# Norm, gating and transposes of each mixer's result inside its out-projection

## The reference

```python
x = x + gate * rms_norm(sublayer(rms_norm(x, g_pre) * (1 + scale) + shift), g_post)
```

```python
# even mixer: two results, one out-projection over both
y_ssd  = rms_norm((ssd(...) + xh * D) * silu(z), norm_w)              # norm over all 1024
y_diff = rms_norm(diff_attention(...), subln_w) * (1 - lam_init)      # norm over each head of 128
out    = concatenate([y_ssd, y_diff]) @ w_out
# odd mixer: retention, then sliding-window attention
y_ret  = rms_norm(retention(...)) * silu(rg)                          # norm over each head of 256
out    = concatenate([y_ret, y_swa]) @ w_out
```

## Time and profile before

| | us |
|---|---|
| median of 3 runs (3827.09 to 3835.24) | 3834.69 |
| the profiled execution, by its own clock outside | 3826.52 |
| its span in the trace | 3824.7 |
| PE busy in it | 3221.2 (84%) |
| DVE busy in it | 2412.0 (63%) |
| ACT busy in it | 1276.7 (33%) |
| POOL busy in it | 575.5 (15%) |

### The profile page before, as it was taken

How to read it: one execution, slowest core, us unless ns; L and a number is a source line. 1 busy time by engine, 2 the same in 40 slices (tenths; PEclk the granted TensorE clock), 3 DMA queues, 4 the chain that set the end, 5 groups by cost and what they waited for, 6 DMA issues and landing times. The chain is left out here.

```text
span 3824.7 us, 41388 instructions
## 1 busy us (share of the span) xinstructions
PE 3221.2 (84%) x14800; PEld 2569.7 (67%) x14800; DVE 2412.0 (63%) x3816; ACT 1276.7 (33%) x2025; POOL 575.5 (15%) x148
## 2 busy tenths in 40 slices
PE   4999967884799895888379789668999898899999
PEld 4766856663676684766367478546887687667887
DVE  6756576897567667689544736466775564465445
ACT  2223224774323323577222514222111322232111
POOL 0000002432000000343100000102444100003443
PEclk9999988997899997899689799888999999769999
DMA  7653526996644452899552033022443251202232
GB/s 247 215 163 127 176 94 228 338 338 222 211 158 143 169 168 91 288 336 338 195 169 73 17 107 127 5 72 78 154 143 110 99 183 63 94 23 80 96 99 77
DMA packets 289773, 584.47 MB, mean 153 GB/s; under 512 B 26034, under 2 KB 134003, under 8 KB 282414
## 3 DMA queue, kind: packets, MB, share of 16 engines
q1 hardware_dynamic: 277610, 537.42, 42.0%
q10 hardware_dynamic: 7364, 27.81, 1.8%
q0 software_dynamic: 4608, 16.78, 1.2%
HBM read 528.93 MB, written 79.76 MB: 159 GB/s over the span
## 5 line engine op out<-in xcount | busy, mean ns | idle before, releaser
L131 ACT CAST w_hi<-ring 128x2048 fp32r<-128x2048 f32 (+2 forms) x172 | 319.3, 1861 | 1276.8 <-PE ps L280 1100.4
L280 PE MATMUL ps<-hT_hi,w_hi 128*128 128x512 f32 (+1 forms) x1256 | 500.4, 398 | 22.8 <-DVEq L898 10.3
L280 PE MATMUL ps<-hT_lo,w_hi 128*128 128x512 f32 (+1 forms) x1256 | 498.4, 397 | 0.0
L138 POOL TENSOR_TENSOR w_lo<-ring,w_hi 128x2048 fp32r<-128x2048 f32 x64 | 307.1, 4799 | 963.3 <-ACTq L2584 466.8
L143 DVE TENSOR_TENSOR w_lo<-ring,w_hi 128x2048 fp32r<-128x2048 f32 (+3 forms) x112 | 245.2, 2195 | 293.3 <-ACT w_hi L131 293.2
L280 PE MATMUL ps<-hT_hi,w_lo 128*128 128x512 f32 (+1 forms) x1256 | 306.9, 396 | 9.4 <-DVE w_lo L143 9.4
L280 PEld LDWEIGHTS ps<-hT_hi,w_hi 128*128 128x128 f32 (+1 forms) x1256 | 238.5, 190 | 82.3 <-DVEq L898 12.0
L280 PEld LDWEIGHTS ps<-hT_hi,w_lo 128*128 128x128 f32 (+1 forms) x1256 | 237.0, 189 | 66.7 <-DVE w_lo L143 10.9
L837 DVE SCALAR_TENSOR_TENSOR piece_sums<-pieces,cond,piece_sums 128x512 f32<-128x512 f32 x294 | 220.8, 751 | 88.9 <-DMA pieces<-in_w_ada_dram 56.1
L280 PEld LDWEIGHTS ps<-hT_lo,w_hi 128*128 128x128 f32 (+1 forms) x1256 | 238.3, 190 | 55.6
L280 PE MATMUL ps<-w_hi,hT_hi 128*128 128x512 f32 (+1 forms) x672 | 259.9, 389 | 1.0 <-ACT w_hi L131 1.0
(11 more groups left out here) (596 smaller groups left out, 6721.6 us busy)
## 6 DMA issues: line engine op xcount, KB each, us to landing
ring<-in_mlp_w_dram SPq DMA_DIRECT2D x64, 1024.0 KB, 5.2
pieces<-in_w_ada_dram SPq DMA_DIRECT2D x96, 512.0 KB, 5.9
ring<-in_w_in_dram SPq DMA_DIRECT2D x36, 1024.0 KB, 7.3
pieces<-in_mod_w_dram SPq DMA_DIRECT2D x72, 512.0 KB, 5.0
raw_sep<-in_w_exp_gate_dram SPq DMA_DIRECT2D x50, 512.0 KB
raw_sep<-in_w_exp_up_dram SPq DMA_DIRECT2D x50, 512.0 KB
raw_sep<-in_w_exp_down_dram SPq DMA_DIRECT2D x24, 1024.0 KB
ring<-in_e_w_in_dram SPq DMA_DIRECT2D x24, 1024.0 KB, 5.5
```

What stands on the lines that cost most here:

```text
L131: self.k.nc.scalar.copy(self.k.parts[0][:, i, 0:words], self.k.ring[:, i, 0:words]).then_inc(self.high, 1)
L138: self.k.nc.gpsimd.tensor_tensor(self.k.parts[1][:, i, 0:words], self.k.ring[:, i, 0:words], self.k.parts[0][:, i, 0:words].bitcast(F32), ...
L280: mm = pe.matmul(out, a if weight_left else b, b if weight_left else a, start=first and part == 0 and q == ks[0] and o == 0, stop=last and ...
```

## The change

`out_projection`, `last_projection`, `gate_rows`, `column_of` and `head_norm_T` are gone. `norm_projection` is one stage that takes the raw result, norms it row tile by row tile (class `Heads`), and multiplies a tile as soon as it is turned.

- The first two weight halves are loaded at the start of the stage before (`load_ahead` in `diff_attention`, `ssd` and `retention`), and ACT casts both to high there (`round_ahead`): in the middle of the 32 units of the attention and of the 16 of the SSD, and at once in the retention. The scratch of the first two moved out of `ring` into its own space.
- In the new stage DVE makes the low parts of the weights and does, per tile: sum of squares per head (places A and B), reciprocal, scale (and gate), and the low part of the turned tile. ACT squares, takes the root and casts high. PE turns a tile in 8 transposes between the two halves of the tile before.
- No warm-up matmuls are left in these three projections.
- In place C the norm's weights come as a row of 1024 for all partitions, and are applied in the scaling; in A they come as a column of 128 by a DMA inside the projection before (`loads`), and are scaled on DVE at the start of the attention.
- In place C the scale and shift rows are loaded after the last tile is turned, and `hand.rows` moves from between the halves of unit 0 to `by_tile`, after tiles 0 and 1 of unit 1 (`late_rows=0`, banks 0 to 3).

```diff
@@ by_tile
     part(1, 1).then_inc(hand.tile_done, 1)
+    if hand.late_rows is not None:
+        pe.wait_ge(hand.row_landed, 64)
+        pe.wait_ge(hand.step, hand.started)
+        pe.wait_ge(hand.y_out, NT)
+        hand.rows(pe, hand.late_rows)
     part(2, 0)
@@ hand_over_on_scalar
     hand.root_y(act, 1)
+    if hand.late_rows is not None:
+        hand.shift_out(act, hand.late_rows)
     hand.square_x(act, 1)
@@ hand_over_on_vector
     sum_of(1)
+    if hand.late_rows is not None:
+        hand.scale_out(dve, hand.late_rows)
     hand.modulate(dve, 0, link)
...
+def round_ahead(k, act, ahead):
+    for i in range(2):
+        act.wait_ge(k.ahead[i], ahead)
+        k.nc.scalar.copy(k.parts[0][:, i, :], k.ring[:, i, :])
...
+    def scaled(self, dve, t):
+        V, y, m = self.k.nc.vector, self.src[:, t, :], self.ms[:, t, :]
+        dve.wait_ge(self.rooted, t + 1)
+        self.link(V.reciprocal(m, m))
+        if self.row is not None:
+            V.scalar_tensor_tensor(y, y, m, self.row, ALU.mult, ALU.mult).then_inc(self.y_made, 1)
+            return
+        ins = V.tensor_tensor(self.per_head(y), self.per_head(y), bcast(m, 2, D // self.nh), ALU.mult)
+        if self.after is not None:
+            self.link(ins)
+            ins = V.tensor_tensor(y, y, self.after[:, t, :], ALU.mult)
+        ins.then_inc(self.y_made, 1)
...
+def norm_projection(k, w, y, first, heads, ahead, next_ahead, hand_of=None):
...
+        def _(act):
+            act.nop().then_inc(W.high, 2)
+            H.square(act, 0)
+            H.root(act, 0)
+            H.square(act, 1)
+            H.high(act, 0)
+            for t in (1, 2):
+                H.root(act, t)
+                H.square(act, t + 1)
+                H.high(act, t)
+            H.root(act, 3)
+            H.high(act, 3)
+            W.split_high(act, 1, 0, 32)
+            W.split_high(act, 1, 1, 32)
...
+            def part(t, i):
+                pe.wait_ge(H.high_out, t + 1)
+                W.high_ready(pe, 0, i)
+                for a, o in ((0, 0), (0, 1), (1, 0)):
+                    if o:
+                        pe.wait_ge(H.low_out, t + 1)
+                    if a:
+                        W.low_ready(pe, 0, i)
+                    for q in range(half):
+                        mm = pe.matmul(k.ps[:, t, :], out[o][:, half * i + q, t * P:(t + 1) * P], wv[i][a][:, q, :], ...
+            H.turn(pe, 0)
+            for t in range(NT):
+                mm = part(t, 0)
+                if t == NT - 1:
+                    mm.then_inc(W.read, 1)
+                else:
+                    H.turn(pe, t + 1)
+                mm = part(t, 1)
+            mm.then_inc(W.read, 1)
...
+        def _(dve):
+            if hand is not None:
+                hand.start(dve)
+                H.gate_in(dve, 0)
+            W.split_low_on_vector(dve, 0, 0)
+            H.total(dve, 0)
+            if hand is not None:
+                H.gate_in(dve, 1)
+                dve.wait_ge(row_in, 16)
+            H.scaled(dve, 0)
+            W.split_low_on_vector(dve, 0, 1)
+            H.low(dve, 0)
+            for t in range(1, NT):
+                H.total(dve, t)
+                if hand is not None and t + 1 < NT:
+                    H.gate_in(dve, t + 1)
+                H.scaled(dve, t)
+                H.low(dve, t)
...
@@ ssd and diff_attention, ACT, in the loop over the units
+                if i == N // 2:
+                    round_ahead(k, act, ahead)
```

More of the change, by code:

```diff
@@ L670, in last_projection @@
-        hand = Handover(k, c, sems[5:], y, out, xh[:, 0:2 * D].rearrange("p (a d) -> p a d", a=2), zz[:, 3 * D:4 * D].rearrange("p (a n) -> p a n", a=2),
-                        zz[:, 0:3 * D], xh[:, 2 * D:4 * D].rearrange("p (a d) -> p a d", a=2))
-        half = KD // 2
+        out = pair_of(nc, c, "normedT", [P, KD, S])
+        H = Heads(k, c, sems[5:15], out=out, **heads)
+        y_done, row_in = sems[15:17]
+        hand, mod = hand_of(c, sems[17:]) if hand_of is not None else (None, None)
@@ L674, in _ @@
+        row = None
+        if hand is not None:
+            y_done = hand.y_out
+            row = c.enter_context(nc.sbuf_tensor(fresh("norm_row"), [P, D], F32))
+            H.row = row[:]
         @block.sync
@@ L676, in _ @@
             W.came_ahead(sp, ahead)
-            hand.load(sp, *mod)
+            if hand is not None:
+                sp.dma_start(row[:], bcast(heads["row"], 0, P)).then_inc(row_in, 16)
             for i in range(2):
                 W.load(sp, 1, i, [(W.raw(i, half, 512), w[:, half * i:half * (i + 1), 512:1024])])
+            if hand is not None:
+                sp.wait_ge(row_in, 16)
+                sp.wait_ge(H.turned, NT)
+                hand.load(sp, *mod)
             sp.wait_ge(W.low, 6)
@@ L689, in _ @@
             W.split_high(act, 1, 1, 32)
-            hand_over_on_scalar(k, act, hand, ahead + 16)
+            if hand is not None:
+                hand_over_on_scalar(k, act, hand, ahead + 16)
+            else:
+                act.wait_ge(W.high, 4)
         @block.tensor
         def _(pe):
[L694 to L700, removed]
@@ L701, in _ @@
-            token_unit(k, pe, W, src, 0, 0, 512, before=rows)
-            pe.wait_ge(hand.row_out, 2)
-            by_tile(k, pe, W, 1, hand, src, KD)
+            pe.nop().then_inc(W.read, 2)
+            wv = [[W.part(a, i, half, 512) for a in range(2)] for i in range(2)]
+            def part(t, i):
[7 more added lines that the diff above has]
+                    for q in range(half):
+                        mm = pe.matmul(k.ps[:, t, :], out[o][:, half * i + q, t * P:(t + 1) * P], wv[i][a][:, q, :],
+                                       start=i == 0 and a == 0 and o == 0 and q == 0, stop=i == 1 and a == 1 and q == half - 1)
+                return mm
@@ L2483, in _ @@
                     V.tensor_copy(taps[:], k.ps[:, 2, 0:80]).then_inc(taps_out, 1)
[L2486 to L2532, removed]
 def mlp(k, w1, w2, hT, y, ahead, side_of=None, mod=None, next_ahead=None, store=None):
@@ L2783, in _ @@
             sp.wait_ge(in_landed, 64)
+            k.load_ahead(sp, next_ahead)
         @block.gpsimd
```

238 lines of the change are left out of this document (113 added, 125 removed).

## The result

The changed kernel takes 3799.57 us (median of 4 runs, 3789.91 to 3805.18) where the kernel before takes 3834.97 (4 runs, 3827.09 to 3840.24). The ratio is 0.9905, with an interval of 0.9890 to 0.9919: 35.4 us less, where 48.4 were forecast. The profiled execution took 3795.96 us, with a span of 3794.2.

A forecast was written before the change was run, and what follows sets the result against it. PE is saturated behind chains of work before three projections, so shortening these shortens the kernel one for one. 14.7 - 2.7 + 12.3 + 29.9 - 5.8 = 48.4 us less, median 3785, range 3768 to 3806.

The forecast's parts named there:

- A: Norm and out-projection after the attention: first unit ends 38.4 us after the stage can start, instead of 53.1; 14.7 less.
- B: Norm and projection after the retention: first unit ends 41.9 us after the stage can start, instead of 54.2; 12.3 less.
- C: Gating, norm and projection after the SSD: first unit ends at 37.8 us instead of 67.7; 29.9 less, 24.1 net.
- rivals 1 and 4: Rival 1, and a fourth: the SSD's hand-over gives back more, all 3.7 lost in the attention, 3792 us; chance 0.08.
- First units: First 96 products of the projections after attention, retention and SSD: end 14.7, 12.3 and 29.9 us sooner.
- C's sum: First unit after the SSD: 16 us, plus 21.8 for the remaining half tiles and two turns, 37.8 in all.
- C's hand-over: Scale and shift rows behind unit 1's first two tiles: VectorE's work 5.3 us later, slower PE 0.5, 5.8 back.
- The upper bound, 10: Most that the hand-over after the SSD could give back: 8.4 + 1.6 us, all that PE loses.
- Attention: Weight casts on ACT delay the next unit's exponentials by 2.5 us, scaling the norm's column adds 0.2: 2.7 back.
- The casts in the SSD and retention loops: Two casts of 1.86 us on ACT: nothing in the retention, 0 in the SSD, at most 0.5 of 3.7.
- Rival 1: The clock falls in the pauses of A and B for two tiles each: 14 us more, 3799; chance 0.15.

The follow-up runs named there:

- the first trace: The profiled execution of the changed kernel's first four runs: it took 3795.96 us, where the median is 3799.57 us.
- the second: The changed kernel run again without any edit, for a second trace: median 3794.0 us.
- the warm start: Changed kernel plus 12 identity products on TensorE ahead of the first turn in each of the three projections: 3785.9 us, ratio 0.9869.
- the tiles ahead: Changed kernel with VectorE summing, scaling and gating tile t+1 before tile t's low part, ScalarE's square and root equally ahead: 3787.8 us.
- A undone: Changed kernel with the stages for the attention's result back to the old way, casts out of the attention: 3808.0 us, ratio 0.9937.
- B undone: Changed kernel with the stages for the retention's result back to the old way: 3796.4 us, ratio 0.9911.
- C undone: Changed kernel with gating, norm, last projection and modulation rows after the SSD back to the old way, no SSD casts: 3800.9 us, ratio 0.9923.

## Why the prediction was right, and where it was not

- **The number.** 3799.6, 3794.0 and 3795.7 us lie inside the stated range (3768 to 3806) and 9 to 15 above the median of 3785. The places themselves gave what was forecast, in part by errors that cancel. The range, made wide for other reasons (rivals 1 and 4), also held a loss that the prediction had not thought of; that is luck.
- **First units.** A 2.6, B 2.1, C 2.2 us shorter than forecast. In A the chain was sized at 7.4 per tile and PE's work at 6.7; they are below 6.58 and 6.44 (24 x 0.233 + 0.85, since the next products start 0.85 behind a turn's start). The single low part of 1024 elements takes 1.28, where I had two of 512 at 1.55; sum and product take 1.21 and 1.23 instead of 1.25 and 1.35. In C's sum the text says six half tiles and adds seven (7 x 2.8 + 2.2 = 21.8); seven is right.
- **C's hand-over.** Forecast 5.8 back; 5.3 with the clock at 2.4 GHz, 11.5 with it falling in the row matmuls, which two of three traces show. The order on VectorE, the wait (3.95 or 7.60 against "5") and the start of `modulate(0)` (12.3 against 12.4) are as argued. The upper bound, 10, was too low: it let PE run slow only behind the rows, and they cost 3.6 more themselves (12.0 for 8.4); the rest of the difference between 5.3 and 11.5 comes behind them.
- **Attention.** Forecast 2.7 back, measured 3.2 to 3.6. The block of 3.70 us stands on ScalarE at 2138.95, and VectorE waits 2.05 behind it, as the prediction said to look for. The casts in the SSD and retention loops are free, as forecast.
- **The step that failed is one that the prediction took for granted:** that the stages behind a place keep their time. They gave back 18.2 us in the first trace and 13.4 in the second. That they did so at a lower granted clock is shown; why the clock falls where it does is open. Rival 1's price was 3799, near the median, but its place was wrong: no tile past the first of A or B ran at half clock. The clock kept 2.4 GHz over pauses of 0.94 us before two turns in B, and fell in stretches tens to hundreds of us behind.
- In B the granted clock is 1.00 behind the first tile, though the loop makes PE wait; in A PE does not wait. The Trainium skill (TensorE: Matmul & The Clock Gate, Loop structure matters more than you think) has a loop in which PE stands idle for 8 us before each product run cold. B's pauses of 0.94 us are far from that, so these traces neither bear it out nor speak against it. After the warming products of the warm start the clock fell behind pauses of 2.37 and 1.21 us.

## What to carry to other kernels

Gains on TensorE's path are not gains of the kernel until the stages behind have been looked at: compare the granted clock of every stretch after the change, also where no code changed, and expect a part back. A matmul block that others wait for (here the scale and shift rows) costs its price at half clock in the range, not at full clock. Undo parts singly, set their sum against the whole (23.3 against 37.3 us here), and look in the traces at which stages moved: with four runs each the medians alone would not have shown that the parts depend on each other. And look at which execution was profiled: where it is the slowest of its kernel, as with the tiles ahead, its stretches don't explain the median.

## What the hardware did that I had not expected

- TensorE's clock fell while the engine was busy without a pause (in C's row matmuls, from 1.05 to 2.0 us for two passes; in the MLP of the changed kernel, where PE is busy without a pause from 2859 to 2939 us and the clock falls at 2925, in the row matmuls again). No wait explains it.
- The pattern mostly repeats: three executions of the changed kernel have the MLP at 424.0 to 424.1 and the window projection at 68.2 to 68.3, though their starts lie up to 6 us apart, and the kernel with A undone shares both to 0.1 us. It does not always: with B undone the code up to the retention is the same, and the MLP took 421.2. The window projection takes one of three times (59.4 to 59.6, 62.2 to 62.4, 67.9 to 68.3), and it went from one to another with an edit some 150 us ahead of it (B undone) or 740 us ahead (C undone). What decides between them is open.
- In the SSD stage the clock rose within the 8.3 us of the warming passes (the next eight passes of its loop take 1.06 us, 1.91 at half clock). With the row matmuls in their place PE worked for 16 us without a pause, and the last couple still took 2.07 us, the time at half clock.
